# A two-layer hybrid decoder trunk: the mixer's side work in another order, and the first feed-forward's table work and transfers moved

## The chip, the cores and the metric

The kernel runs on one core of a Trainium2 chip. It is one launch. The metric is device microseconds (us) from start to end of it, and of several runs the median is taken.

## The reference

Everything is fp32: 256 positions, width 1024, two layers. What each layer computes:

```
x = x + 0.5 * swiglu(rms_norm(x, ffn1_norm), w_gate, w_up, w_down)      # D_FF = 2816
x = x + hybrid_mixer(rms_norm(x, mix_norm))
x = x + 0.5 * swiglu(rms_norm(x, ffn2_norm), w_gate2, w_up2, w_down2)

hybrid_mixer(h):
    proj = h @ w_in                 # splits: qkv, z, beta, a | s5_u | lru_x, lru_y | ret q, k, v, g | 4 gates of 1024
    A = gated delta rule (chunks of 64, a 64x64 triangular solve a head and chunk, a state of 64x64)
    B = s5_layer: complex diagonal scan over 16 groups of 64 states, gelu, then a GLU
    C = RG-LRU: a gated linear recurrence over 256 channels
    D = retention: rotary q and k, scores * decay mask, group norm, swish gate
    merged = sum_b sigmoid(gate_b) * (branch_b @ w_branch[b])
    return merged @ w_out
```

## The kernel before

The weights are what the time goes to. They arrive as some 400 pieces of 128x1024 (512 KB; some 448 KB) in HBM order of use. SyncE starts the transfer of piece i into one of three `raw` slots once VectorE has finished with piece i-3. ScalarE copies the piece, rounded to the matmul's format, into `whi` (L1026), VectorE writes the rest `raw - whi` into `wlo` (L1442; some late pieces go to GpSimd, L1357), and TensorE multiplies twice with `whi` and once with `wlo` (L487 to L489; the 16 units of gates L557 to L559, with 512 columns a matmul). So each piece takes about 2.7 us of TensorE, 1.0 of ScalarE and 1.2 of VectorE.

TensorE's order is written out by hand, and so are those of ScalarE and VectorE; the engines are in order, and each waits by semaphore counts. `split_to(i)` and `ahead(unit)` stand on ScalarE and VectorE for "bring the copies (or rests) up to piece i", so what is written between two of these delays the pieces behind it.

A layer has the stages FFN1 (22 units `gu1_0` to `gu1_21` of a gate and an up half, then `dn1`), the mixer (projections, gate units `g0` to `g15`, merges `mg0` to `mg7`, `wo`), and FFN2. FFN1 also carries work on the S5 parameters, which is small and dependent: four exponentials and an absolute value on ScalarE (L1139 to L1144, which need another activation table than silu does), a scan and two chains for an angle on VectorE, later the tables `tmpF`, `ret` of powers (`turn_tables`, L1583).

In the mixer the small matmuls of the four branches stand between gate units. Each writes one of four PSUM banks in the order of the table `SIDE`: a unit can only start when the unit four places earlier in the table was taken by the engine that the table names. The names used below: `eb`, `gb`, `bb` (decays and betas; L716, L734; taken as `dec` by VectorE L1800), `ktr`, `vtr` (transposed keys and values, L724, taken by VectorE L1778 to L1784), `kk`, `qk` (keys and queries against keys, L748, taken by VectorE L1816, L1819), `pq0` to `pq7` (input of S5's pairs of states, `s5_in`, taken by `s5_state` on VectorE, L1828 to L1837, then turned back on GpSimd, L1383 to L1387, and summed by `s5_out`), the units of the six levels of the triangular inverse (L815, L816 among them), `rotq`, `rotk`, `sc0` to `sc3`, `ro`, `rm`, `rv2` (rotation, scores, output, mean and variance of retention), `u`, `w`, `ws`, `su`, `oi`, `oa`, `gs` (delta rule; L893 is a product with new values, L1886 on VectorE makes these values).

Of the kernel before, what the change touches and what calls it, by code (L numbers as in the profile page):

```python
# [32 lines left out]
ALU = mybir.AluOpType  # L33
ACT = mybir.ActivationFunctionType
# [42 lines left out]
EARLY = CCOLS["bo"][0]  # L77

# [62 lines left out]
for _name, _n, _ in STREAM:  # L141
# [8 lines left out]
           if _n.startswith("mg") or _n in [f"g{_k}.1" for _k in range(11, 16)] + ["wo0.0", "wo1.0"]]  # L150
# [7 lines left out]
LEVEL_UNITS = ([[("x0_0", "act"), ("y0_0", "act"), ("x1_0", "act"), ("y1_0", "act"), ("t0_1", "act")]]  # L158
               + [[(f"{n}{hp}_{lv}", "act") for hp in range(2) for n in ("y", "xt")] for lv in range(1, LEVELS - 1)]
               + [[(f"yt0_{LEVELS - 1}", "act"), (f"y1_{LEVELS - 1}", "act")]])  # L160
SIDE = ([("lr", "act"), ("li", "act"), ("l2q", "act"), ("l2k", "act"), ("rowt", "act"), ("eb", "act"),
         ("ktr", "dve"), ("vtr", "dve")]
        + [("gb0", "dve"), ("bb0", "act"), ("gb1", "dve"), ("bb1", "act")]
        + [(n, "dve") for n in ("kk0", "kk1", "qk0", "qk1")]
        + [u for lv in range(LEVELS) for u in
           (LEVEL_UNITS[lv]
            + [(f"pq{s}", "dve") for s in ([2 * lv, 2 * lv + 1] if lv < 4 else [])]
            + ([("rotq", "dve"), ("rotk", "dve")] if lv == 4 else []))]
        + [("u", "act"), ("w0", "act"), ("w1", "act"),
           ("su0", "dve"), ("sc0", "dve"), ("sc1", "dve"),  # L170
           ("ws1", "dve"), ("oi1", "act"), ("su1", "dve"), ("sc2", "dve"), ("sc3", "dve"),
           ("ws2", "dve"), ("oi2", "act"), ("su2", "dve"), ("ro", "act"),
           ("ws3", "dve"), ("oi3", "act"), ("glu", "act"), ("rm", "dve"),
           ("oa0", "dve"), ("oa1", "dve"), ("gs", "act"), ("rv2", "act")])
# [43 lines left out]
def trunk(nc, weights, params, consts, positions, x_in, y_out):  # L218
    ctx = ExitStack()
    with ctx:  # L220
# [81 lines left out]
        scm = big[:, 16 * SEQ:16 * SEQ + 4 * 384].rearrange("p (h c) -> p h c", h=4)  # L302
# [158 lines left out]
        def sync_layer(sp):  # L461
            for i in range(max(Now.layer * NP, RAW_SLOTS), (Now.layer + 1) * NP):
                sp.wait_ge(*low_ready(i - RAW_SLOTS))
                sp.dma_start(landing(i), weight_piece(i)).then_inc(once[f"raw{i % RAW_SLOTS}"], 16)
                if i == 10:
                    sp.dma_start(par[:, NORMS:], layer_params(0)[:, NORMS:]).then_inc(S("par"), 16)
                if i == 16:
                    sp.dma_start(cst[:, EARLY:], consts[:, EARLY:]).then_inc(once["tables_load"], 16)
                if Now.layer + 1 < DEPTH and i == piece_at("dn2_0.0"):
                    sp.wait_ge(*since("hh", MF + MF // 2))  # L470
                    sp.wait_ge(*since("scaled", 2 * KD))
                    Now.layer += 1
                    sp.dma_start(par[:], layer_params(Now.layer)).then_inc(S("par"), 16)
                    Now.layer -= 1

        def tensor_layer(pe):
# [195 lines left out]
            pe.wait_ge(once["tables_load"], 16)  # L672
# [39 lines left out]
            ps = side_bank("eb")  # L712
            for t in range(2):
                for hp in range(2):
                    h = 2 * t + hp
                    last = mm(ps[64 * hp:64 * hp + 64, t * SEQ:(t + 1) * SEQ], ident[0:32, h:h + 1].to_broadcast([32, 64]), rows[0:32], start=True, stop=True)  # L716
            last.then_inc(S("side"), 1)
            gate(0)
            pe.wait_ge(S("k_normed"), 1)
            for unit, q0 in (("ktr", 2), ("vtr", 4)):  # L720
                ps = side_bank(unit)
                for j in range(2):
                    for t in range(2):
                        last = nc.tensor.transpose(ps[:, j * 256 + t * P:j * 256 + (t + 1) * P], qkv[:, q0 + t, j * P:(j + 1) * P], ident)  # L724
                last.then_inc(S("side"), 1)

            def decays_and_betas(hp):

                both = [(side_bank(f"gb{hp}"), 0), (side_bank(f"bb{hp}"), 32)]
                for t in range(2):  # L730
                    h = 2 * t + hp
                    for n, r in enumerate(chunks):
                        for ps, row in both:
                            last = mm(halves(ps[r, t * P:(t + 1) * P]), ident[row:row + 32, row + h:row + h + 1].to_broadcast([32, 64]),  # L734
                                      rows[row:row + 32].rearrange("p (j n c) -> p j n c", j=2, n=2)[:, :, n, :], start=True, stop=True)
                            if (t, n) == (1, 1):
                                last.then_inc(S("side"), 1)

# [12 lines left out]

            decays_and_betas(0)
            decays_and_betas(1)
            gate(1)
            against_k("kk", 2)
            against_k("qk", 0)
            gate(2)
            gate(3)
# [20 lines left out]

            pe.wait_ge(S("main_act"), main.taken("su"))  # L780
            def first_pair(hp):

                pe.wait_ge(S("y_first"), hp + 1)
                xs, ys = side_bank(f"x{hp}_0"), side_bank(f"y{hp}_0")
                for i in range(4):
                    t, j = i // 2, i % 2
                    for ps, swapped in ((xs, False), (ys, True)):
                        for r, out in zip(chunks, others):
                            if swapped:
                                last = mm(ps[out, i * 64:(i + 1) * 64], ident[r, r], mt[r, hp, t, j, :], start=True, stop=True)  # L790
                            else:
                                last = mm(ps[r, i * 64:(i + 1) * 64], mt[r, hp, t, j, :], ident[r, r], start=True, stop=True)
                        if i == 3:
                            last.then_inc(S("side"), 1)
# [33 lines left out]

            pe.wait_ge(once["masks"], 4)
            for hp in range(2):  # L830
                first_pair(hp)
                gate_part(4, hp)
            middle(side_bank("t0_1"), 0, 1, "x0_0")
            s5_in((0, 1))
            for lv in range(1, LEVELS - 1):
                gate_part(4 + lv, 0)
                ps = both_sides(0, lv, f"xt1_{lv - 1}" if lv > 1 else "t0_1")
                middle(ps, 1, lv, f"xt1_{lv - 1}" if lv > 1 else "x1_0")
                if lv >= 2:
                    s5_out(2 * lv - 4)  # L840
                    s5_out(2 * lv - 3)
# [3 lines left out]
                if lv < 4:  # L845
                    s5_in((2 * lv, 2 * lv + 1))
                if lv == 4:

                    pe.wait_ge(S("main_act"), main.taken("rv"))
                    for unit, src in (("rotq", rq), ("rotk", rk)):  # L850
                        ps = side_bank(unit)
                        for t in range(2):
                            last = mm(ps[:, t * SEQ:(t + 1) * SEQ], cst_("perm"), src[:, t, :], start=True, stop=True)
                        last.then_inc(S("side"), 1)
            lv = LEVELS - 1
            gate_part(4 + lv, 0)
            ps = side_bank(f"yt0_{lv}")
            inverse_rows(ps, 0, f"xt1_{lv - 1}")
            middle(ps, 1, lv, f"xt1_{lv - 1}")
            s5_out(2 * lv - 4)  # L860
            s5_out(2 * lv - 3)
            gate_part(4 + lv, 1)
            inverse_rows(side_bank(f"y1_{lv}"), 1, f"yt0_{lv}").then_inc(S("side"), 1)
            gate(10)

# [44 lines left out]
            def scores(h):  # L910
                t, r = h // 2, slice(64 * (h % 2), 64 * (h % 2) + 64)
                ps = side_bank(f"sc{h}")
                mm(ps[:, 0:SEQ], rk[r, t, 0:P], rq[r, t, :], start=True, stop=True)
                mm(ps[:, SEQ:384], rk[r, t, P:SEQ], rq[r, t, P:SEQ], start=True, stop=True).then_inc(S("side"), 1)

            def means(unit, src):

                ps = side_bank(unit)
                for t in range(2):
                    last = mm(ps[:, t * SEQ:(t + 1) * SEQ], bo, src[:, t, :], start=True, stop=True)  # L920
                last.then_inc(S("side"), 1)


            gate_part(11, 0)
            state_up(0)
            pe.wait_ge(S("rotated"), 2)
            scores(0)
            scores(1)
# [3 lines left out]
            scores(2)  # L932
            scores(3)
            gate_part(12, 0)
            from_state(2)
            state_up(2)

            pe.wait_ge(S("side_dve"), side.taken("sc3"))
            ps = side_bank("ro")
            for t in range(2):  # L940
                for j in range(2):
                    for hp, r in enumerate(chunks):
                        h = 2 * t + hp
                        v = slice(h * DH, (h + 1) * DH)
                        if j == 0:
                            mm(ps[r, t * SEQ:(t + 1) * SEQ], rv[:, 0, v], scm[:, h, 0:SEQ], start=True, stop=False)
                        else:
                            last = mm(ps[r, t * SEQ + P:(t + 1) * SEQ], rv[:, 1, v], scm[:, h, SEQ:384], start=False, stop=True)
            last.then_inc(S("side"), 1)
# [9 lines left out]
            pe.wait_ge(S("side_act"), side.taken("ro"))  # L959
            means("rm", tmpB)  # L960
# [13 lines left out]
            pe.wait_ge(S("ro_sq"), 1)  # L974
            means("rv2", tmpC)
# [33 lines left out]
        def scalar_layer(act):  # L1009
# [71 lines left out]
            def stack_masks():  # L1081

                act.wait_ge(once["tables_load"], 16)
# [52 lines left out]
            silus(1, range(0, 4))  # L1136
# [126 lines left out]
            ahead("g1")  # L1263
            for hp in range(2):
# [937 lines left out]
```

## Time and profile before

| what | value |
|---|---|
| time, median of 3 runs | 1316.59 us (1313.99 to 1317.89) |
| the profiled execution, its own time | 1312.74 us |
| its span | 1311.0 us |
| TensorE busy | 1281.6 us, 98% of the span |
| VectorE, ScalarE, GpSimd busy | 919.6, 673.2, 236.7 us |
| mean granted clock of TensorE | 0.994 of full speed |
| DMA | 220.14 MB, 168 GB/s on average |

The profile is of one execution, so its durations are compared with 1312.74 us, not with the median. Busy TensorE time counts matmuls that overlap, and includes stretches at half clock. The waits list says for which engine's instruction an idle engine waited.

### The profile page before, as it was taken

What the parts mean: (1) busy time and instruction counts of PE and PEld (TensorE: products, weight loads), DVE (VectorE), ACT (ScalarE), POOL (GpSimd) and SP (SyncE); (2) the same over time, 40 slices, a digit from 0 to 9 for tenths busy, and PEclk for the clock granted to TensorE, in tenths of its full rate; (3) what the DMA queues carried; (4) which work ended last, traced back from release to release, by engine and by line L of the source; (5) the groups of instructions that cost most, each with busy time, mean ns of one, the idle gap of its engine ahead of it and who ended that gap; (6) DMA issues with size and microseconds to landing.
All of it is one profiled execution on the core that took longest, in us unless ns stands there. A gap on an engine that the chain in (4) does not pass through costs nothing.

```text
span 1311.0 us, 25653 instructions
## 1 busy us (share of the span) xinstructions
PE 1281.6 (98%) x10848; PEld 1199.3 (91%) x10848; DVE 919.6 (70%) x1383; ACT 673.2 (51%) x991; POOL 236.7 (18%) x183
## 2 busy tenths in 40 slices
PE   9999999999999999999999999999999999999997
PEld 9999999987777899999999999999777778999997
DVE  5788675896967766666658885567879487566654
ACT  6544647654335465444554446477444445544542
POOL 1000011006834410000100000100366363000000
PEclk9999999999999999999999999999999999999999
DMA  6756564544242655566646556545423355555562
GB/s 204 245 186 194 183 200 145 166 149 141 86 139 99 178 175 194 187 211 209 193 147 200 175 187 206 170 154 169 159 85 113 97 161 186 166 189 185 173 218 91
DMA packets 92178, 220.14 MB, mean 168 GB/s; under 512 B 6944, under 2 KB 48160, under 8 KB 91680
## 3 DMA queue, kind: packets, MB, share of 16 engines
q1 hardware_dynamic: 92064, 218.50, 52.0%
q8 instruction: 86, 1.41, 0.4%
q14 instruction: 28, 0.23, 0.1%
HBM read 217.42 MB, written 1.05 MB: 167 GB/s over the span
## 4 chain that ended last, share of the span: by engine, by line
PE 79%; DVE 14%; ACT 3%; issue 2%; DMA 2%; POOL 0%; SPq 0%; DVEq 0%; ACTq 0%
PE bank L487 21%; PE bank L489 21%; PE bank L488 21%; DVE wlo L1442 4%; PE bank L557 3%; PE bank L558 3%; PE bank L559 3%; DMA raw<-weights 1%; DVE bank L1829 1%; DVE tmpA L1828 1%; PE bank L997 1%; PE bank L998 1%; PE bank L999 1%; ACT whi L1026 1%; DVE bank L1831 1%
## 5 line engine op out<-in xcount | busy, mean ns | idle before, releaser
L1442 DVE TENSOR_TENSOR wlo<-raw,whi 128x1024 fp32r<-128x1024 f32 (+1 forms) x384 | 475.1, 1260 | 237.4 <-ACT whi L1026 235.4
L1026 ACT ACTIVATE whi<-raw 128x1024 fp32r<-128x1024 f32 (+1 forms) x414 | 421.1, 1037 | 195.2 <-DMA raw<-weights 117.3
L487 PE MATMUL bank<-xh,whi 128*128 128x256 f32 x1744 | 489.2, 281 | 5.4 <-DVE wlo L1442 4.9
L488 PE MATMUL bank<-xl,whi 128*128 128x256 f32 x1744 | 486.8, 279 | 0.0
L489 PE MATMUL bank<-xh,wlo 128*128 128x256 f32 x1744 | 486.7, 279 | 0.0
L487 PEld LDWEIGHTS bank<-xh,whi 128*128 128x128 f32 x1744 | 327.8, 188 | 7.3 <-issue 6.7
L488 PEld LDWEIGHTS bank<-xl,whi 128*128 128x128 f32 x1744 | 327.8, 188 | 0.1
L489 PEld LDWEIGHTS bank<-xh,wlo 128*128 128x128 f32 x1744 | 327.8, 188 | 0.0
L487 PE MATMUL bank<-hh,whi 128*128 128x256 f32 x704 | 196.8, 280 | 0.0
L489 PE MATMUL bank<-hh,wlo 128*128 128x256 f32 x704 | 196.5, 279 | 0.0
L488 PE MATMUL bank<-hl,whi 128*128 128x256 f32 x704 | 196.5, 279 | 0.0
L1394 POOL TENSOR_TENSOR flat<-flat 128x256 f32<-128x256 f32 x36 | 35.6, 988 | 743.8 <-ACT flat L1052 742.9
L1110 ACT ACTIVATE tmpB<-tmpB 128x256 f32<-128x256 f32 x88 | 36.6, 417 | 219.3 <-DVE tmpB L1490 219.3
L487 PEld LDWEIGHTS bank<-hh,whi 128*128 128x128 f32 x704 | 132.3, 188 | 0.2 <-issue 0.2
L488 PEld LDWEIGHTS bank<-hl,whi 128*128 128x128 f32 x704 | 132.3, 188 | 0.0
L489 PEld LDWEIGHTS bank<-hh,wlo 128*128 128x128 f32 x704 | 132.3, 188 | 0.0
L557 PE MATMUL bank<-whi,xh 128*128 128x512 f32 x256 | 107.3, 419 | 2.1 <-DVE wlo L1442 2.1
L558 PE MATMUL bank<-wlo,xh 128*128 128x512 f32 x256 | 101.8, 398 | 0.0
L559 PE MATMUL bank<-whi,xl 128*128 128x512 f32 x256 | 101.6, 397 | 0.0
L1357 POOL TENSOR_TENSOR wlo<-raw,whi 128x1024 fp32r<-128x1024 f32 x30 | 73.7, 2469 | 73.6 <-ACT whi L1026 73.5
L1490 DVE TENSOR_TENSOR tmpB<-bank,invb 128x256 f32<-128x256 f32 x88 | 37.2, 423 | 58.1 <-PE bank L489 56.9
L557 PEld LDWEIGHTS bank<-whi,xh 128*128 128x128 f32 x256 | 48.6, 190 | 22.0 <-DVE wlo L1442 6.1
(408 smaller groups left out, 1558.1 us busy)
## 6 DMA issues: line engine op xcount, KB each, us to landing
raw<-weights SPq DMA_DIRECT2D x350, 512.0 KB, 3.8
raw<-weights SPq DMA_DIRECT2D x64, 448.0 KB, 4.0
cst<-consts SPq DMA_DIRECT2D x1, 1088.0 KB, 7.2
par<-params SPq DMA_DIRECT2D x1, 1072.5 KB, 7.2
par<-params SPq DMA_DIRECT2D x1, 1060.5 KB, 7.5
x<-x_in SPq DMA_DIRECT2D x2, 512.0 KB, 6.6
y_out<-ret SPq DMA_DIRECT2D x4, 256.0 KB, 2.1
ropec<-positions SPq DMA_DIRECT2D x1, 128.0 KB, 7.8
```

The source lines that it names most:

```text
L487: mm(out, w[0], a[0], start=start, stop=False)
L488: mm(out, w[0], a[1], start=False, stop=False)
L489: return mm(out, w[1], a[0], start=False, stop=stop)
L557: mm(in_four(ps), xh[:, k, t], wh[:, n, :], start=(k == 0), stop=False)
L558: mm(in_four(ps), xh[:, k, t], wl[:, n, :], start=False, stop=False)
L559: last = mm(in_four(ps), xl[:, k, t], wh[:, n, :], start=False, stop=(k == KD - 1))
L1026: A(slot(whi, i), slot(raw, i), ACT.Copy).then_inc(once["high"], 1)
L1110: A(tmpB[:, m % 2, :], tmpB[:, m % 2, :], ACT.Silu).then_inc(S(f"silu{f}"), 1)
L1357: tt(slot(wlo, i), slot(raw, i), r32(slot(whi, i)), ALU.subtract).then_inc(S("low_pool"), 1)
L1394: tt(squared[:, 0, :], squared[:, 0, :], squared[:, k, :], ALU.add).then_inc(S("sq_step" if k < KD - 2 else "sq_added"), 1)
L1442: V.tensor_tensor(slot(wlo, i), slot(raw, i), r32(slot(whi, i)), ALU.subtract).then_inc(S("low_dve"), 1)
L1490: V.tensor_tensor(tmpB[:, m % 2, :], main.bank(f"gu{f}_{m}")[:, 0:SEQ], invb, ALU.mult).then_inc(S("gated"), 1)
```

## The change

**Transfers.** In layer 0 the rest of the parameters (1060 KB in one transfer behind piece 10) and the tables (1088 KB in one transfer behind piece 16) are cut: the small parameters go behind piece 6, the rest in four parts behind pieces 12, 14, 16, 18, the tables in four parts behind 20, 22, 24, 26.

**FFN1.** ScalarE's exponentials stand one piece pair earlier, the last of them with the silu after it ahead of the pieces that it followed; the two angle chains on VectorE are interleaved; the powers (L1583) of part 1 are moved from before unit 13 into it, and later ones follow.

**Mixer.** The table `SIDE` and the written orders of TensorE, ScalarE and VectorE change together: decays before keys and values, S5's first pair ahead of gate unit 2, one state of S5 after each rest, retention's scores in level 5 and its output and norm right behind, the first and the last branch together.

The diff, cut to its core:

```diff
+LATE_PARAMS = _in_parts(12, 2, MATRICES, NPAR, 4)
+LATE_TABLES = _in_parts(20, 2, EARLY, NCST, 4)
...
-SIDE = ([("lr", "act"), ("li", "act"), ("l2q", "act"), ("l2k", "act"), ("rowt", "act"), ("eb", "act"),
-         ("ktr", "dve"), ("vtr", "dve")]
-        + [("gb0", "dve"), ("bb0", "act"), ("gb1", "dve"), ("bb1", "act")]
-        + [(n, "dve") for n in ("kk0", "kk1", "qk0", "qk1")]
...
+         ("gb0", "dve"), ("bb0", "act"), ("gb1", "dve"), ("bb1", "act"), ("ktr", "dve"), ("vtr", "dve")]
+        + [(n, "dve") for n in ("kk0", "kk1", "qk0", "qk1", "pq0", "pq1")]
...
@@ TensorE
-            decays_and_betas(0)
-            decays_and_betas(1)
             gate(1)
             against_k("kk", 2)
             against_k("qk", 0)
+            pe.wait_ge(S("main_act"), main.taken("su"))
+            s5_in((0, 1))
             gate(2)
             gate(3)
...
+            pe.wait_ge(S("rotated"), 2)
+            scores(0)
+            scores(1)
+            gate_part(9, 0)
...
+            scores(2)
+            scores(3)
+            gate_part(9, 1)
+            inverse_rows(side_bank("y1_5"), 1, "yt0_5").then_inc(S("side"), 1)
+            retained()
             gate(10)
+            pe.wait_ge(S("side_act"), side.taken("ro"))
+            means("rm", tmpB)
@@ ScalarE, FFN1
-            silus(1, range(0, 4))
+            silus(1, range(0, 3))
...
             A(ly_, lq, ACT.Exp, scale=-1.0).then_inc(S("pexp"), 1)
+            ahead("gu1_3")
             act.wait_ge(S("pmul"), 1)
             A(sm["mag"], sm["lrdt"], ACT.Exp).then_inc(S("pexp"), 1)
-            silus(1, range(4, 8))
+            silus(1, range(3, 8))
@@ VectorE, FFN1
             turn_tables(0)
-            turn_tables(1)
             for m in range(13, MF):
                 up(1, [m])
-                for part in {16: (5, 6), 17: (7,), 18: (8,), 19: (9, 10), 20: (11,), 21: ()}.get(m, (m - 11,)):
+                for part in {17: (5, 6), 18: (7,), 19: (8, 9), 20: (10, 11), 21: ()}.get(m, (m - 12,)):
                     turn_tables(part)
@@ VectorE, mixer
+            below(0)
+            below(1)
             dve.wait_ge(S("side"), side.ready("ktr"))
-            dve.wait_ge(S("side_act"), side.taken("rowt"))
...
             dve.wait_ge(S("tables"), 2)
+            s5_state(0)
             ahead("g3")
-            for lv in range(LEVELS):
-                for hp in range(2):
-                    split_to(last_piece(f"g{4 + lv}") + 2 + hp)
-                if lv < 4:
-                    s5_state(2 * lv)
-                    s5_state(2 * lv + 1)
...
+            s5_state(1)
+            for lv in range(LEVELS - 1):
+                split_to(last_piece(f"g{4 + lv}") + 2)
+                if lv < 3:
+                    s5_state(2 * lv + 2)
+                split_to(last_piece(f"g{4 + lv}") + 3)
+                if lv < 3:
+                    s5_state(2 * lv + 3)
+                if lv == 3:
+                    rotate()
...
             ahead("g11")
             state_up(0)
-            masked(0)
-            masked(1)
...
             values(1)
             state_up(1)
-            masked(2)
-            masked(3)
...
+            ahead("g14")
             link(V.tensor_tensor(go, go, tmpD, ALU.mult))
             link(V.scalar_tensor_tensor(go, go, gnh, zz, ALU.mult, ALU.mult))
             branch(0, go)
-            ahead("g14")
-
-            dve.wait_ge(S("side_act"), side.taken("rv2"))
-            link(V.reciprocal(tmpC, tmpC))
-            link(V.tensor_tensor(tmpB, tmpB, tmpC, ALU.mult))
```

How the rows of an engine stand, in the order in which it takes them (line numbers are those of each kernel; L1026 before is L1042 after, L1442 is L1464, L557 to L559 are L568 to L570). First ScalarE in FFN1 of layer 0, from the silu of unit 2 on. Before:

```order
L1110 ACTIVATE tmpB<-tmpB 128x256
L1104 ACTIVATE hh<-tmpC 128x256
L1026 ACTIVATE whi<-raw 128x1024 x2
L1110 ACTIVATE tmpB<-tmpB 128x256
L1104 ACTIVATE hh<-tmpC 128x256
L1139 ACT_TABLE_LOAD
...
L1142 ACTIVATE small<-small 128x2
L1144 ACTIVATE small<-small 128x8
L1026 ACTIVATE whi<-raw 128x1024 x2
L1110 ACT_TABLE_LOAD
```

And of the changed kernel, from the same silu:

```order
L1126 ACTIVATE tmpB<-tmpB 128x256
L1120 ACTIVATE hh<-tmpC 128x256
L1155 ACT_TABLE_LOAD
...
L1158 ACTIVATE small<-small 128x2
L1042 ACTIVATE whi<-raw 128x1024 x2
L1161 ACTIVATE small<-small 128x8
L1126 ACT_TABLE_LOAD
L1126 ACTIVATE tmpB<-tmpB 128x256
L1120 ACTIVATE hh<-tmpC 128x256
L1042 ACTIVATE whi<-raw 128x1024 x2
```

The first four exponentials and their table load moved from behind unit 3's silu to behind unit 2's, ahead of the copies of pieces 8 and 9; the last exponential, the load back and unit 3's silu now stand ahead of pieces 10 and 11.

Second TensorE in the mixer, from the small matmuls behind gate unit 0 to the start of gate unit 2. Before:

```order
L724 MATMUL bank<-cst,qkv 128x128 x8
L734 MATMUL bank<-rows,cst 64x128 x16
L557 MATMUL bank<-whi,xh 128x512
...
L559 MATMUL bank<-whi,xl 128x512
L748 MATMUL bank<-qkv 64x64 x32
L557 MATMUL bank<-whi,xh 128x512
```

And changed:

```order
L730 MATMUL bank<-rows,cst 64x128 x8
L749 MATMUL bank<-cst,qkv 128x128 x8
L568 MATMUL bank<-whi,xh 128x512
...
L570 MATMUL bank<-whi,xl 128x512
L761 MATMUL bank<-qkv 64x64 x32
L771 MATMUL bank<-su,par 128x256 x4
L568 MATMUL bank<-whi,xh 128x512
```

Half of the decay matmuls went ahead of gate unit 0, the other half ahead of the transposes, and the four matmuls of S5's first pair stand directly behind those of `kk` and `qk`.

Third VectorE in the mixer, from a rest of gate unit 1 on. Before (L1778 takes `ktr`, L1800 the decays, L1811 and L1812 mask them, L1816 and L1819 take `kk` and `qk`):

```order
L1442 TENSOR_TENSOR wlo<-raw,whi 128x1024
L1778 TENSOR_TENSOR qkvp<-bank,rowT 128x256
...
L1784 SCALAR_TENSOR_TENSOR qkvp<-bank,rowT 128x256 x2
L1442 TENSOR_TENSOR wlo<-raw,whi 128x1024
L1800 TENSOR_SCALAR big<-bank,rowT 128x64 x8
...
L1442 TENSOR_TENSOR wlo<-raw,whi 128x1024 x2
L1811 TENSOR_TENSOR big<-big,cst 128x256
...
L1816 SCALAR_TENSOR_TENSOR big<-bank,big 128x256 x2
L1819 TENSOR_TENSOR big<-bank,big 128x256 x2
L1442 TENSOR_TENSOR wlo<-raw,whi 128x1024 x6
```

And changed:

```order
L1464 TENSOR_TENSOR wlo<-raw,whi 128x1024
L1811 TENSOR_SCALAR big<-bank,rowT 128x64 x8
L1826 TENSOR_TENSOR qkvp<-bank,rowT 128x256
...
L1832 SCALAR_TENSOR_TENSOR qkvp<-bank,rowT 128x256 x2
L1464 TENSOR_TENSOR wlo<-raw,whi 128x1024
...
L1464 TENSOR_TENSOR wlo<-raw,whi 128x1024 x2
L1850 TENSOR_TENSOR big<-big,cst 128x256
...
L1855 SCALAR_TENSOR_TENSOR big<-bank,big 128x256 x2
L1858 TENSOR_TENSOR big<-bank,big 128x256 x2
L1464 TENSOR_TENSOR wlo<-raw,whi 128x1024 x2
L1867 TENSOR_TENSOR tmpA<-bank,wide 128x512
```

The eight instructions on decays moved from behind to ahead of those on `ktr` and `vtr`, and S5's first state stands after two rests where it stood after six.

## Rows read from the trace of the kernel before

**Rows 1.** The page: span, busy time of the engines, chain that ended last.
```profile
span 1311.0 us, 25653 instructions
...
PE 1281.6 (98%) x10848; PEld 1199.3 (91%) x10848; DVE 919.6 (70%) x1383; ACT 673.2 (51%) x991; POOL 236.7 (18%) x183
...
PE 79%; DVE 14%; ACT 3%; issue 2%; DMA 2%; POOL 0%; SPq 0%; DVEq 0%; ACTq 0%
```

**Rows 2.** Waits of TensorE: engine, line, waited for: total us, times, longest us.
```profile
PE bank L487 <- DVE wlo L1442: 4.9, 6, 1.8
PE bank L734 <- DVE qkvp L1784: 3.3, 2, 1.7
...
PE bank L893 <- DVE big L1886: 2.6, 2, 1.3
PE bank L557 <- DVE wlo L1442: 2.1, 3, 0.9
...
PE bank L815 <- DVE tmpC L1836: 0.4, 2, 0.2
```

**Rows 3.** TensorE in both FFN1: start, us, engine, line, op, tiles, count, [idle before, releaser].
```profile
42.48 0.35 PE L487 MATMUL bank<-xh,whi 128*128 128x256 f32 x1 [1.80 <-DVE wlo L1442]
...
93.66 0.35 PE L487 MATMUL bank<-xh,whi 128*128 128x256 f32 x1 [0.54 <-DVE wlo L1442]
...
686.01 0.36 PE L487 MATMUL bank<-xh,whi 128*128 128x256 f32 x1 [0.70 <-DVE wlo L1442]
...
738.07 0.36 PE L487 MATMUL bank<-xh,whi 128*128 128x256 f32 x1 [1.41 <-DVE wlo L1442]
```

**Rows 4.** Timeline of ScalarE at the parameter work of layer 0.
```profile
36.68 0.42 ACT L1110 ACTIVATE tmpB<-tmpB 128x256 f32<-128x256 f32 x1 [1.63 <-DVE tmpB L1490]
...
37.44 1.28 ACT L1139 ACT_TABLE_LOAD   x1
...
39.72 1.99 ACT L1026 ACTIVATE whi<-raw 128x1024 fp32r<-128x1024 f32 x2
```

**Rows 5.** Timeline of VectorE: parameter work (layer 0), turned tables (layer 1).
```profile
38.17 0.69 DVE L1558 TENSOR_TENSOR_SCAN tmpF<-cst 128x256 f32<-128x256 f32 x1 [0.87 <-DMA par<-params]
...
734.34 2.32 DVE L1583 TENSOR_SCALAR ret<-tmpF,small 128x256 f32<-128x256 f32 x8
```

**Rows 6.** Timeline of TensorE at the products of keys and queries, layer 0.
```profile
285.64 0.67 PE L734 MATMUL bank<-rows,cst 32*64 32x128 f32 x16 [1.65 <-DVE qkvp L1784]
...
292.04 1.16 PE L748 MATMUL bank<-qkv 64*64 64x64 f32 x64
```

**Rows 7.** Timeline of VectorE in the same stretch.
```profile
285.42 1.22 DVE L1442 TENSOR_TENSOR wlo<-raw,whi 128x1024 fp32r<-128x1024 f32 x1
...
290.01 2.35 DVE L1442 TENSOR_TENSOR wlo<-raw,whi 128x1024 fp32r<-128x1024 f32 x2
...
293.99 0.76 DVE L1816 SCALAR_TENSOR_TENSOR big<-bank,big 128x256 f32<-128x256 f32 x2
```

**Rows 8.** Timeline of VectorE: one level of the triangular inverse, beside GpSimd.
```profile
321.08 3.91 DVE L1442 TENSOR_TENSOR wlo<-raw,whi 128x1024 fp32r<-128x1024 f32 x2
```

**Rows 9.** Timeline of VectorE: delta-rule state and branch sums, layer 0.
```profile
385.72 2.30 DVE L1905 SCALAR_TENSOR_TENSOR tmpE<-tmpE,su 128x512 f32<-128x512 f32 x1
387.94 1.21 DVE L1442 TENSOR_TENSOR wlo<-raw,whi 128x1024 fp32r<-128x1024 f32 x1
...
411.31 3.42 DVE L1442 TENSOR_TENSOR wlo<-raw,whi 128x1024 fp32r<-128x1024 f32 x1
```

**Rows 10.** Windows of TensorE: us, busy (count), granted clock, DMA share, GB/s.
```profile
284.50:288.00 3.50, 2.35 (x24) 1.00 0.53 161
...
390.40:393.80 3.40, 3.40 (x19) 0.50 0.93 303
...
926.30:929.70 3.40, 1.74 (x29) 1.00 0.30 83
929.70:933.10 3.40, 3.40 (x22) 0.50 0.63 208
```

More of the change, by code:

```diff
@@ L737, in decays_and_betas @@
                                 last.then_inc(S("side"), 1)
+            ps = side_bank("eb")
+            for t in range(2):
+                for hp in range(2):
+                    h = 2 * t + hp
+                    last = mm(ps[64 * hp:64 * hp + 64, t * SEQ:(t + 1) * SEQ], ident[0:32, h:h + 1].to_broadcast([32, 64]), rows[0:32], start=True, stop=True)
+            last.then_inc(S("side"), 1)
+            decays_and_betas(0)
+            gate(0)
+            decays_and_betas(1)
+            pe.wait_ge(S("k_normed"), 1)
+            for unit, q0 in (("ktr", 2), ("vtr", 4)):
+                ps = side_bank(unit)
+                for j in range(2):
+                    for t in range(2):
+                        last = nc.tensor.transpose(ps[:, j * 256 + t * P:j * 256 + (t + 1) * P], qkv[:, q0 + t, j * P:(j + 1) * P], ident)
+                last.then_inc(S("side"), 1)
             def against_k(name, q0):
@@ L827, in inverse_rows, with rotated @@
                 return last
-            pe.wait_ge(once["masks"], 4)
[L830 to L834, printed above, removed]
+            def rotated():
+                pe.wait_ge(S("main_act"), main.taken("rv"))
+                for unit, src in (("rotq", rq), ("rotk", rk)):
+                    ps = side_bank(unit)
+                    for t in range(2):
+                        last = mm(ps[:, t * SEQ:(t + 1) * SEQ], cst_("perm"), src[:, t, :], start=True, stop=True)
+                    last.then_inc(S("side"), 1)
@@ new lines, in scores, with means @@
+            def scores(h):
+                t, r = h // 2, slice(64 * (h % 2), 64 * (h % 2) + 64)
+                ps = side_bank(f"sc{h}")
+                mm(ps[:, 0:SEQ], rk[r, t, 0:P], rq[r, t, :], start=True, stop=True)
+                mm(ps[:, SEQ:384], rk[r, t, P:SEQ], rq[r, t, P:SEQ], start=True, stop=True).then_inc(S("side"), 1)
+            def means(unit, src):
+                ps = side_bank(unit)
+                for t in range(2):
+                    last = mm(ps[:, t * SEQ:(t + 1) * SEQ], bo, src[:, t, :], start=True, stop=True)
+                last.then_inc(S("side"), 1)
@@ L931, in tensor_layer @@
             state_up(1)
-            scores(2)
-            scores(3)
             gate_part(12, 0)
             from_state(2)
+            pe.wait_ge(S("ro_sq"), 1)
+            means("rv2", tmpC)
             state_up(2)
[L938 to L949, printed above, removed]
             gate_part(12, 1)
@@ L1653, in vector_layer @@
             up(1, [11])
+            dve.wait_ge(once["tables_load"], TABLE_LOADS)
             cr, ci = halves(par_("scr"), 8), halves(par_("sci"), 8)
```

293 lines of the change are left out of this document (151 added, 142 removed).

## The prediction

> **What bounds the kernel now.** I read the page first [rows 1]: TensorE is busy 1281.6 of 1311.0 us, and four fifths of the chain that ended last are its matmuls. The change removes no matmul, so it can only move what TensorE waits for, and the half-clock stretches. Next the list of TensorE's waits [rows 2]: the reader is to see that no class is above 4.9 us, that the rests `wlo` from VectorE lead it, and that three classes lie where the change works: L734 behind the transposed values (3.3), L893 behind the delta rule's values (2.6), gates behind `wlo` (2.1). Then the timelines around each [rows 3 to 9], and the windows with the granted clock [rows 10]: behind some of these waits the clock stands at 0.50 for 3.4 us, and that is counted as busy. A dense stretch of 3.4 us at half clock does 1.7 us of work, so each costs up to 1.7 us, as much as the wait ahead of it.
>
> The sum is made against the profiled execution, 1312.74 us (span 1311.0 and 1.7 around it). It is 3.85 below the median 1316.59; I take the difference found in it off the median.
>
> **FFN1, ScalarE.** In layer 0 piece 10's rest holds TensorE up by 1.80 us until 42.48 [rows 3]. Its copy starts at 39.72, behind the table load of 1.28 at 37.44 and the five small functions, 2.28 in all [rows 4]. Afterwards load and four functions stand ahead of the copies of pieces 8 and 9. That shifts piece 8's rest to about 35.5, some 0.6 behind where TensorE wants it, a new wait. Then the last exponential needs the scan and a product on VectorE (scan 0.69, [rows 5]) behind gate and up of unit 3, so it comes at about 38.6; behind it now come the load back (1.28), the silu and its product (0.42 each, overlapping to 0.8 [rows 4]), and only then piece 10's copy, 40.7 to 41.6, and its rest until 42.9. So TensorE goes on at 43.03: 0.55 later than at present. In layer 1 the same order gives 687.05 for 686.01, +1.04.
>
> **FFN1, later.** In layer 1, eight L1583 take 2.32 us straight ahead of a rest for which TensorE waits 1.41 [rows 3, 5]. Four of the eight move behind it: half of 2.32 is 1.16; as a rest's start also frees the next transfer earlier, I take 1.2 to 1.57, -1.4. In layer 0 the wait of 0.54 at 93.66, goes, and with it 0.16 us of refilling (my value between nothing and the 0.35 that the first matmul takes [rows 3]): -0.70. FFN1 sum: 0.55 - 0.70 + 1.04 - 1.4 = **-0.5**. Interleaving the angle chains shortens VectorE's dependent work beside it, which TensorE doesn't wait for. The split transfers I cost at nothing: TensorE waits for no weight transfer there, and the tables' last part lands about 2 us before VectorE's first use. If that cover were gone, the price is up to a 1 MB transfer's worth of delay of that first use, some microseconds once; bounds 0 and +2.
>
> **Mixer, the decays.** Now VectorE takes `ktr` and `vtr`, and L734 waits 1.65 for it (1.66 in layer 1) until 285.64 [rows 2, 6]. With the decays split to both sides of gate unit 0, gate unit 1 can start at 285.4 instead of 286.2. But the eight decay instructions (some 1.6 us) now stand ahead of a rest that was done at 286.6 [rows 7] and will be at 288.4, when TensorE wants it at 288.3. So `kk` and `qk` end at 292.45 and not at 293.1.
>
> **Mixer, S5's first pair.** It needs the banks of `kk0` and `kk1`, four places earlier in the table. VectorE takes them in L1816, at 293.99 to 294.75 [rows 7], at the end of work without a gap: two rests until 292.3, four masks, then the pair. Nothing of that is moved away, and it starts 0.2 later. TensorE is there at 292.45 and the banks are free at 294.95, so it waits 2.6 us, where it now goes straight on with gate unit 2. Gate unit 2 starts at 296.2 for 293.1: +3.0, of which 1.06 are the four matmuls of the pair, moved from later. Net **+1.97** in layer 0. In layer 1 the present kernel has a half-clock window right behind the 1.66 wait (the one at 929.7 [rows 10]), which costs gate unit 1 some 1.1 and L734 0.46; the changed order breaks that wait up: net **+0.43**.
>
> **Mixer, the levels.** VectorE takes two rests in 3.91 us beside GpSimd's rotation back, against 1.21 for one alone [rows 8, 9]; L815 then waits 0.2 at a time, three times a layer [rows 2]. One state behind each rest spreads that; two waits of 0.3 remain by my replay. **-0.3** a layer (bounds -0.9 and +0.5). The Trainium skill, GPSIMD Engine Reference (the table of the engine's properties), says GpSimd's SBUF interfaces are shared with VectorE, with contention for instructions with two SBUF inputs. The trace agrees (`wlo` reads two: 3.91 against 2 x 1.21). By that rule respacing saves none of the stretching, only the queueing, and the sum would have 0 here in place of -0.3.
>
> **Mixer, state and retention.** At L893 TensorE waits 1.3 a layer for values that stand behind masks, L1905 (2.30, slowed) and a rest (1.21) [rows 2, 9]. The masks go to level 5 and L1905 behind the second values: -1.46 with the refill, +0.4 for small waits in the new order. Behind that wait comes a window at 0.50 (at 390.4 [rows 10]), and one alike in layer 1: -1.75 and -1.5. Sum **-2.8** and **-2.55**.
>
> **Mixer, the end.** A rest of 3.42 us beside GpSimd [rows 9] holds a gate up by 0.95 [rows 2]; a branch's six instructions ahead of it go behind the next one. **-1.1** a layer; my replay leaves it 0.5 us of margin.
>
> **Clock.** Does the new wait of 2.6 us bring a half-clock window of its own? For: windows with little work (1.74 of 3.40 busy, small matmuls) are followed by 0.50 [rows 10]. Against: 2.35 busy of 3.50 around the same kind of wait kept 1.00 [rows 10]; and the wait sits between dense gates. A window with 2.6 idle in it has less than either. It is not shown by any row, so from below 0, from above 1.7 a layer; between them I take 0.7, as one of two layers falls. The Trainium skill, TensorE: Matmul & The Clock Gate (Part 1, and its passage on oscillation), says that the throttled clock is the default, that activity releases it, and that waits between bursts bring it back. The trace agrees in kind (926.3, then 929.7 [rows 10]). By the rule alone both layers fall, which is the second rival below.
>
> Sum: FFN1 -0.5; layer 0: 1.97 - 0.3 - 2.8 - 1.1 = -2.2; layer 1: 0.43 - 0.3 - 2.55 - 1.1 = -3.5; clock +1.4 over both. **-4.8**, so 1316.6 - 4.8 = 1311.8.
>
> **Rivals.** (1) No new half-clock window: -6.2, 1310.4. For it speaks the 284.5 row; 0.22.
> (2) Both layers fall at full price (+3.4 for 1.4), and of what is removed about 1 us shows up again at the next unit, as TensorE is then nearer to VectorE's chain: -1.8, 1314.8, no change that can be told. The 926.3 row speaks for it; 0.20.
> (3) The banks are free in time, because VectorE's earlier work is drawn forward with the decays: the pair costs nothing, 2.6 less in each layer and no clock in question: about -10, 1306.5. Against it: VectorE's chain there has no gap [rows 7]; 0.08.
> (4) Slower. VectorE becomes the bound in the levels: L815 already waits 0.2 in those with two states [rows 2], so VectorE has nothing to spare there, and the new order puts rotation and scores into levels that were light. If every one of twelve levels takes x longer, the result is -4.8 + 12x; no gain from x = 0.4, slower by over 0.3% from x = 0.73. At x = 0.8 the time is 1316.6 + 4.8 = 1321.4. A rest slowed by 1.5 once per level [rows 8] would do it. Against: what waits there now is 0.2 a time, three times a layer, so x is so far 0.1 at most; 0.10.
> The forecast itself (one window falls) has 0.40.
>
> **Numbers.** 0.3% (3.95 us) is about what a measurement can tell: faster is below 1312.6. The forecast lies just below it, so 0.24 of its 0.40 go to faster, 0.16 to same. Rival 1 gives 0.18 to faster and 0.04 to same, rival 2 0.18 to same and 0.02 to slower, rival 3 0.08 to faster, rival 4 0.10 to slower. Faster 0.50, same 0.38, slower 0.12. The range leaves out half of rival 3 and most of rival 4, and takes in the bounds of transfers and levels: 1306.5 to 1318.5. The forecast's own is 1309.5 to 1314.
>
> **What would show it.** Right: S5's first pair (L771) waits about 2.6 us for L1855 in both layers; L893's successor, the product with new values, waits under 0.4; the gate at 414.8 has no wait; piece 10's copy in FFN1 comes behind the silu, and TensorE's wait there is some 0.6 plus 1.8; one window at 0.50 near the pair, none near the states. Wrong: no wait at L771; windows at 0.50 in the levels; L815-like rows that wait over 0.7 us in each level; a wait for the tables ahead of the scr products in FFN1.

## The result

The changed kernel takes 1318.56 us (median, 1312.8 to 1321.91, 18 runs) against 1314.89 of the kernel before (1310.6 to 1317.89, 18 runs): a ratio of 1.0025, 95% interval 1.0015 to 1.0035. It is 3.3 us slower, where 4.8 faster was forecast. The profiled execution took 1318.7, at its median; that of before (1312.74) had been 2.2 under its own.

The page of the changed kernel (span, busy time, chain that ended last), beside [rows 1]:

```profile
span 1316.6 us, 25674 instructions
...
PE 1278.7 (97%) x10848; PEld 1197.4 (91%) x10848; DVE 933.4 (71%) x1383; ACT 677.0 (51%) x995; POOL 236.0 (18%) x183
...
PE 78%; DVE 13%; ACT 4%; DMA 2%; issue 2%; POOL 0%; SPq 0%; DVEq 0%; ACTq 0%
```

TensorE is busy 2.9 us less and the span is 5.6 longer: the loss is idle time. VectorE is busy 13.8 us more with as many instructions. That is the clue: something made the same instructions longer. TensorE's waits, beside [rows 2] (who waited for what: total, times, longest):

```profile
PE bank L1013 <- DVE tmpA L2004: 7.3, 2, 3.7
PE bank L771 <- DVE big L1855: 5.0, 2, 2.5
PE bank L498 <- DVE wlo L1464: 4.7, 6, 1.5
...
PE bank L749 <- DVE big L1811: 1.4, 2, 0.9
PE bank L943 <- DVE big L1943: 1.3, 2, 0.7
...
PE bank L730 <- ACT egb L1279: 0.9, 1, 0.9
```

The waits at L734 and L815 are gone, though 1.4 comes back at the transposes (L749, behind the decays) and 0.9 once at L730, where L734 was; that of the values (L893 before, L943 now) fell from 2.6 to 1.3, S5's pair (L771) waits 2.5 a layer as worked out. But the first row is new and in no step of the prediction: 3.7 us a layer at a merge.

To see where time goes, the matmuls with weights are counted in both traces; their order is the same. Start of number k in us, before and changed, first layer:

```
   k   what                         before   changed  difference
   0   first                         10.64     10.17     -0.48
  75   early in FFN1                 20.69     20.71     +0.03
2160   gate unit 1                  286.24    285.30     -0.94
2184   gate unit 2                  293.13    296.46     +3.33
2190   six matmuls on               294.63    299.18     +4.55
2496   gate unit 15                 414.79    412.20     -2.59
2538   second half of merge 1       424.69    425.82     +1.13
2544   six matmuls on               426.09    428.55     +2.46
```

At gate unit 15 the changed kernel leads by 2.6 us, S5's wait and its half clock included (the 0.48 of the start is gone 75 matmuls on). Then it loses 5.05 within 48 matmuls, and the second layer repeats that (0.36 behind at the same gate, 5.40 forty-eight matmuls on, 5.59 at the end). The place, on VectorE:

```profile
408.75 1.22 DVE L1464 TENSOR_TENSOR wlo<-raw,whi 128x1024 fp32r<-128x1024 f32 x1
409.89 2.90 DVE L1988 TENSOR_TENSOR ly<-ly,tmpD 128x512 f32<-128x512 f32 x1
412.82 1.67 DVE L1989 SCALAR_TENSOR_TENSOR ly<-ly,small,zz 128x512 f32<-128x512 f32 x1
414.52 2.52 DVE L1835 CAST brh<-ly 128x512 fp32r<-128x512 f32 x1
417.07 2.79 DVE L1836 TENSOR_TENSOR brl<-ly,brh 128x512 fp32r<-128x512 f32 x1
419.78 2.63 DVE L1835 CAST brh<-tmpB 128x512 fp32r<-128x512 f32 x1
422.45 2.72 DVE L1836 TENSOR_TENSOR brl<-tmpB,brh 128x512 fp32r<-128x512 f32 x1
425.09 0.67 DVE L2004 SCALAR_TENSOR_TENSOR tmpA<-wide,bank 128x512 f32<-128x512 f32 x1
```

and on GpSimd in the same stretch (an `x2` or `x3` is a group):

```profile
409.58 2.65 POOL L1379 TENSOR_TENSOR wlo<-raw,whi 128x1024 fp32r<-128x1024 f32 x1 [7.20 <-ACT whi L1042]
412.19 1.74 POOL L1388 TENSOR_TENSOR brl<-tmpF,brh 128x512 fp32r<-128x512 f32 x1
413.90 5.42 POOL L1379 TENSOR_TENSOR wlo<-raw,whi 128x1024 fp32r<-128x1024 f32 x2
419.62 7.78 POOL L1379 TENSOR_TENSOR wlo<-raw,whi 128x1024 fp32r<-128x1024 f32 x3 [0.31 <-ACT whi L1042]
```

Read them in pairs: L1988 ends at 412.79, 0.56 behind the end of GpSimd's first (412.23); L1989 at 414.49, 0.56 behind 413.93; the last subtraction at 425.17, 0.55 behind the end of the second of GpSimd's three (424.62). One VectorE instruction goes through per GpSimd instruction. Before, four of the six began ahead of GpSimd's first and took their own time; the other branch's conversion met GpSimd and took 2.50 already then:

```profile
408.73 0.69 DVE L1936 TENSOR_TENSOR ly<-ly,tmpD 128x512 f32<-128x512 f32 x1
409.46 0.75 DVE L1937 SCALAR_TENSOR_TENSOR ly<-ly,small,zz 128x512 f32<-128x512 f32 x1
410.25 0.43 DVE L1787 CAST brh<-ly 128x512 fp32r<-128x512 f32 x1
410.70 0.69 DVE L1788 TENSOR_TENSOR brl<-ly,brh 128x512 fp32r<-128x512 f32 x1
...
411.06 2.59 POOL L1357 TENSOR_TENSOR wlo<-raw,whi 128x1024 fp32r<-128x1024 f32 x1 [8.93 <-ACT whi L1026]
```

That also accounts for VectorE's busy time: the six took 5.75 before and take 15.2 now, and the rest that took 3.42 takes 1.22, so 7.3 more a layer and 14.5 in both, against 13.8 for the whole kernel.

L2004 is what frees the first merge's bank. It stands behind both branches on VectorE, TensorE needs that bank (a ring of three) for the second half of merge 1 (`mg1`), and waits:

```profile
425.82 0.80 PE L1013 MATMUL bank<-whi,brh 128*128 128x512 f32 x1 [3.66 <-DVE tmpA L2004]
```

S5's pair, and windows of TensorE around it and around this wait (us, busy, granted clock, DMA):

```profile
295.08 1.45 PE L771 MATMUL bank<-su,par 32*128 32x256 f32 x8 [2.51 <-DVE big L1855]
...
294.60:298.00 3.40, 2.92 (x12) 0.67 0.44 146
298.00:301.40 3.40, 3.40 (x14) 0.83 0.76 232
...
422.40:425.80 3.40, 0.00 (x0) 0.95 0.51 159
425.80:429.20 3.40, 3.38 (x9) 0.55 0.62 189
```

Both waits are followed by a stretch at the lower level, in both layers. The 0.67 and 0.83 are one such stretch cut by the windows' edges: from 295.8 to 299.2 the granted clock is 0.50.

### The profile page after: what moved, and what is told of

It is laid out like the page before. It is cut to its first block, busy times and chain, and to the rows that moved or that the text cites. A ratio compares the mean times of both kernels' runs of the same rounds, so it can differ in the third digit from the quotient of the medians.

```text
span 1316.6 us, 25674 instructions
## 1 busy us (share of the span) xinstructions
PE 1278.7 (97%) x10848; PEld 1197.4 (91%) x10848; DVE 933.4 (71%) x1383; ACT 677.0 (51%) x995; POOL 236.0 (18%) x183
## 4 chain that ended last, share of the span: by engine, by line
PE 78%; DVE 13%; ACT 4%; DMA 2%; issue 2%; POOL 0%; SPq 0%; DVEq 0%; ACTq 0%
PE bank L498 20%; PE bank L500 20%; PE bank L499 20%; DVE wlo L1464 4%; PE bank L568 4%; PE bank L570 3%; PE bank L569 3%; DMA raw<-weights 1%; ACT whi L1042 1%; DVE qkv L1741 1%; DVE brh L1835 1%; PE bank L819 1%; PE bank L1013 1%; PE bank L771 1%; PE bank L1014 1%
## 5 line engine op out<-in xcount | busy, mean ns | idle before, releaser
L1464 DVE TENSOR_TENSOR wlo<-raw,whi 128x1024 fp32r<-128x1024 f32 (+1 forms) x384 | 471.1, 1249 | 233.5 <-ACT whi L1042 231.5
L1042 ACT ACTIVATE whi<-raw 128x1024 fp32r<-128x1024 f32 (+1 forms) x414 | 420.1, 1036 | 203.8 <-DMA raw<-weights 91.4
L568 PE MATMUL bank<-whi,xh 128*128 128x512 f32 x256 | 107.2, 419 | 1.0 <-DVE wlo L1464 0.9
L570 PE MATMUL bank<-whi,xl 128*128 128x512 f32 x256 | 102.2, 399 | 0.0
L568 PEld LDWEIGHTS bank<-whi,xh 128*128 128x128 f32 x256 | 48.9, 191 | 19.0 <-issue 4.9
```

Of the source, the lines that this page charges most:

```text
L568: mm(in_four(ps), xh[:, k, t], wh[:, n, :], start=(k == 0), stop=False)
L570: last = mm(in_four(ps), xl[:, k, t], wh[:, n, :], start=False, stop=(k == KD - 1))
L1042: A(slot(whi, i), slot(raw, i), ACT.Copy).then_inc(once["high"], 1)
L1464: V.tensor_tensor(slot(wlo, i), slot(raw, i), r32(slot(whi, i)), ALU.subtract).then_inc(S("low_dve"), 1)
```

## The experiments

The theory: VectorE's conversions, and its subtractions and products of two SBUF operands, wait for the GpSimd instruction in flight; the new order put six of them beside GpSimd's rests, so the first merge's bank comes free late. Rivals: order alone (too much work ahead of L2004), the FFN1 part, or S5's pair. Each ratio is to runs of the kernel before on the same chip.

**FFN1 part alone**: the kernel before with the diff's transfers and its FFN1 pieces on ScalarE and VectorE.

```diff
-                if i == 10:
+                if i in LATE_PARAMS:
...
-            silus(1, range(0, 4))
+            silus(1, range(0, 3))
```

> The kernel before with the change to FFN1 and the transfers alone, the mixer as it was. My sums: layer 0 -0.15, layer 1 -0.4 to -0.65, so about 0.5 to 0.8 us under before; TensorE's wait for the rest of piece 10 at 1.5 and a new one of 0.5 ahead of it, the wait at 93.7 gone. The rival, that the split transfers or the moved tables cost in layer 1 (the profile of the changed kernel has three waits of 0.3 to 0.9 early in the mixer of layer 1), expects +1 to +2 us and those waits again.

1313.45 us, 0.9990 (0.9976 to 1.0003) of before. The sum of -0.5 lies inside the interval (-3.2 to +0.4 us), +1 to +2 outside it. The early waits in layer 1's mixer are there too, but also in `before_halves` below, which has none of the change; they go with a weight transfer that took longer in those executions (ScalarE waited 3.31 and 2.79 for that piece, 1.95 in the kernel before, 3.34 in `transfers_alone` below). Why it took longer was not tried.

**Mixer part alone**: all other pieces of the diff, and none of these.

```diff
+            s5_in((0, 1))
             gate(2)
...
+            ahead("g14")
             link(V.tensor_tensor(go, go, tmpD, ALU.mult))
```

> The kernel before with the mixer's new order alone. If the loss is in the mixer's end and in S5's first pair, as the profile of the changed kernel says: a wait of 3.7 at the third merge and of 2.5 at S5's pair in each layer, each with a half-clock stretch behind it, and +3 to +5 us against before. If the FFN1 part makes the loss: no change to 2 us faster than before.

1318.89 us, 1.0031 (1.0017 to 1.0046): +4.1, with waits of 3.6 and 2.5 a layer at the two places. The loss is the mixer's.

**VectorE makes two more rests**, so GpSimd starts later.

```diff
-           if _n.startswith("mg") or _n in [f"g{_k}.1" for _k in range(11, 16)] + ["wo0.0", "wo1.0"]]
+           if _n.startswith("mg") or _n in [f"g{_k}.1" for _k in range(11, 14)] + ["wo0.0", "wo1.0"]]
```

> The changed kernel, but the rests of the pieces g14.1 and g15.1 are made by VectorE (2 x 1.2 us more a layer on it) and no longer by GpSimd, so that GpSimd stands still while VectorE works on the branches. My theory, that each of VectorE's conversions and subtractions waits there for the GpSimd instruction in flight: the six instructions that take 1.7 to 2.9 us go back to 0.4 to 0.8, the wait of 3.7 at the third merge is gone or below 1, and its half-clock stretch with it: 7 to 10 us faster than the changed kernel, about 4 to 7 faster than before. The rival, that the order of the work alone makes the third merge late (too much work on VectorE ahead of the first merged sum): the wait stays or grows by the 2.4 us more.

1307.83 us, 0.9954 (0.9938 to 0.9971): 6.0 under before, so 9.3 under the changed kernel by the two ratios. VectorE has 2.4 us a layer more to do, and the wait at the merge is gone. Four of the six are short again; the two that still meet GpSimd's rests of merges (411.22 to 413.69 and 414.81 to 417.28) are not:

```profile
411.35 2.89 DVE L1988 TENSOR_TENSOR ly<-ly,tmpD 128x512 f32<-128x512 f32 x1
414.27 0.75 DVE L1989 SCALAR_TENSOR_TENSOR ly<-ly,small,zz 128x512 f32<-128x512 f32 x1
415.06 2.51 DVE L1835 CAST brh<-ly 128x512 fp32r<-128x512 f32 x1
417.60 0.69 DVE L1836 TENSOR_TENSOR brl<-ly,brh 128x512 fp32r<-128x512 f32 x1
418.21 0.42 DVE L1835 CAST brh<-tmpB 128x512 fp32r<-128x512 f32 x1
418.66 0.69 DVE L1836 TENSOR_TENSOR brl<-tmpB,brh 128x512 fp32r<-128x512 f32 x1
```

The rival of too much work is refuted.

**S5's first pair behind gate unit 2**, its first state behind the rests that follow.

```diff
+            gate(2)
             pe.wait_ge(S("main_act"), main.taken("su"))
             s5_in((0, 1))
-            gate(2)
             gate(3)
...
-            s5_state(0)
             ahead("g3")
+            s5_state(0)
             s5_state(1)
```

> The changed kernel, with S5's first pair on TensorE behind gate unit 2 in place of ahead of it, and its first state on VectorE behind the rests of gate unit 3. The wait of 2.5 and the half-clock stretch behind it (1.6) should go in both layers: 6 to 8 us faster than the changed kernel. The rival, that TensorE then waits as long at the next unit, since VectorE's chain is late as a whole: under 2 us faster, and a new wait of 1 to 2.5 at gate unit 3 or in the first level.

1313.93 us, 0.9999 (0.9983 to 1.0014), so 3.4 under the changed kernel: between the two. The wait of 2.5 is gone, and part of it comes back in the first level, where the ring of banks wants the second state taken:

```profile
310.81 0.27 PE L800 MATMUL bank<-cst,big 64*64 64x64 f32 x2 [1.50 <-DVE tmpD L1875]
```

Behind this wait the granted clock stayed at 1.00 in layer 0 (310.8 to 317.6) and was 0.50 in layer 1 (954.2 to 957.6).

**GpSimd's rests in halves**: same elements, two instructions.

```diff
-                    tt(slot(wlo, i), slot(raw, i), r32(slot(whi, i)), ALU.subtract).then_inc(S("low_pool"), 1)
+                    n = slot(wlo, i).shape[-1] // 2
+                    tt(slot(wlo, i)[:, 0:n], slot(raw, i)[:, 0:n], r32(slot(whi, i)[:, 0:n]), ALU.subtract)
+                    tt(slot(wlo, i)[:, n:], slot(raw, i)[:, n:], r32(slot(whi, i)[:, n:]), ALU.subtract).then_inc(S("low_pool"), 1)
```

> The changed kernel, with each of GpSimd's rests made by two instructions of half the length. The same elements and bytes pass on GpSimd. My theory, that a conversion or subtraction of VectorE waits for the end of the one GpSimd instruction in flight: its time beside GpSimd falls from 2.5 to 2.9 to about 1.3 to 1.7 us, the six of them from about 15 to 9 us, and the wait of 3.7 at the third merge goes to nothing, -6 to -9 us against the changed kernel. The rival, that both engines share a port access by access: VectorE's instructions keep 2.5 to 2.9 us, the wait stays at 3.7 and the time within 1 us of the changed kernel.

1308.48 us, 0.9941 (0.9926 to 0.9956) of before, 11 under the changed kernel, more than the 6 to 9 expected. This tells the two forms of contention apart. VectorE in this kernel:

```profile
408.00 1.79 DVE L1990 TENSOR_TENSOR ly<-ly,tmpD 128x512 f32<-128x512 f32 x1
409.83 1.67 DVE L1991 SCALAR_TENSOR_TENSOR ly<-ly,small,zz 128x512 f32<-128x512 f32 x1
411.53 1.40 DVE L1837 CAST brh<-ly 128x512 fp32r<-128x512 f32 x1
412.97 1.67 DVE L1838 TENSOR_TENSOR brl<-ly,brh 128x512 fp32r<-128x512 f32 x1
```

and GpSimd:

```profile
407.73 1.51 POOL L1380 TENSOR_TENSOR wlo<-raw,whi 128x512 fp32r<-128x512 f32 x1 [6.10 <-ACT whi L1042]
409.21 1.73 POOL L1381 TENSOR_TENSOR wlo<-raw,whi 128x512 fp32r<-128x512 f32 x1
...
418.89 1.29 POOL L1380 TENSOR_TENSOR wlo<-raw,whi 128x512 fp32r<-128x512 f32 x1
```

The halves take 1.29 undisturbed and 1.5 to 1.75 beside VectorE, and TensorE now waits 0.6 twice for GpSimd's halves. Six instructions of VectorE take 9.7 us in place of 15.2, all of them done at 417.8 where it was 425.2, and the wait is gone.

**The first branch ahead of gate unit 15's rest again.**

```diff
-            ahead("g14")
             link(V.tensor_tensor(go, go, tmpD, ALU.mult))
             link(V.scalar_tensor_tensor(go, go, gnh, zz, ALU.mult, ALU.mult))
             branch(0, go)
+            ahead("g14")
             branch(3, tmpB)
```

> The changed kernel, with the first branch (product, norm, conversion, subtraction) ahead of gate unit 14's rest again, as before the change; GpSimd keeps its rests. Theory: of those four, two to three still meet GpSimd's instruction, which starts at 409.6, so the rest of g14.0 comes at 414 to 416 and is wanted at 412.2: the wait of 3.7 at the merge goes, one of 2 to 4 comes at gate unit 14; -1 to -5 us against the changed kernel. The rival, that the new place of the branch alone made the loss: no wait over 1 us at either place, -8 to -10 us.

(The rest that `ahead("g14")` brings is that of piece g15.0; the expectation calls it g14.0. Its "third merge" is the second half of merge 1.) 1324.21 us, 1.0057 (1.0040 to 1.0073): slower than the changed kernel, outside both expectations. Two instructions meet GpSimd, and the rest behind them too:

```profile
412.12 2.51 DVE L1835 CAST brh<-ly 128x512 fp32r<-128x512 f32 x1
414.66 1.63 DVE L1836 TENSOR_TENSOR brl<-ly,brh 128x512 fp32r<-128x512 f32 x1
416.22 3.36 DVE L1464 TENSOR_TENSOR wlo<-raw,whi 128x1024 fp32r<-128x1024 f32 x1
```

so gate unit 15 starts at 419.63 after a wait of 5.39. The mechanism was right and the size missed: I had not counted the slowed rest itself (2.1 us). So this part of the old order costs still more in the new surroundings. What differs from before is when GpSimd's rests fall: its first began 2.33 behind the branch's first product then (408.73 and 411.06), and 0.96 behind it here (410.61 and 411.57).

**Both cures together** (`own_rests` and `pair_later`).

> The changed kernel with VectorE making its own rests (as in own_rests) and S5's first pair behind gate unit 2 (as in pair_later). If the two are independent, the gains add: 1307.8 less 4 to 5, so 1303 to 1304.5, with the wait of 1.5 at the first level that pair_later showed. The rival, that VectorE becomes late at the end by the two rests more once TensorE is earlier: above 1306.

1304.99 us, 0.9913 (0.9897 to 0.9929): just above the expected 1303 to 1304.5. By the ratios 14.7 under the changed kernel, where 9.3 and 3.4 make 12.7: they add, within what the intervals can tell.

**S5's first state in VectorE's idle time**, as above but:

```diff
+            split_to(last_piece("g3") + 2)
             s5_state(0)
             ahead("g3")
             s5_state(1)
```

> As both, but S5's first state ahead of the rest of piece g4.1, where VectorE stands idle for 1.4 us in pair_later and which TensorE wants 3 us later. The wait of 1.5 at the first level should fall to about 0.5, and the half-clock stretch behind it (1.7) may go: 1300 to 1302. The rival, that any wait among those small matmuls brings the half clock: 1303, with a window at 0.50 there.

1303.12 us, 0.9899 (0.9882 to 0.9916). The wait at L800 is 0.7 once, in place of 1.5 twice; the time is 1 to 3 above what was expected. It is the rival's 1303, but without the rival's sign: the granted clock at these matmuls was 1.00, as it was in `both` behind its waits of 1.5. That this run is faster than `both` (0.9899 and 0.9913) is within the intervals.

**Halves in the kernel before**, with none of the change.

> The kernel before, with each of GpSimd's rests made by two instructions of half the length, and nothing of the change. If VectorE waits for GpSimd's instruction in flight there too, its rest of 3.42 at 411.3 falls to about 2 and the wait of 0.95 a layer goes: 1 to 3 us faster than before. Then the new order with the same cure (halves, 8.8 under before in its comparison) is worth 6 to 8 of it. The rival, that the shorter instructions alone are worth the 8.8: before_halves comes out 7 to 10 us faster as well.

1315.91 us, 0.9998 (0.9985 to 1.0011): no change, less than expected. The wait at gate unit 15 goes, but the merge waits 0.7 twice in its place, and matmuls wait 0.7 twice for GpSimd's halves (L1359):

```profile
PE bank L487 <- DVE wlo L1444: 5.0, 6, 2.1
PE bank L734 <- DVE qkvp L1786: 3.3, 2, 1.7
...
PE bank L997 <- DVE tmpA L1962: 1.5, 2, 0.7
PE bank L487 <- POOL wlo L1359: 1.3, 2, 0.7
```

So the halves are worth nothing without the new order, and with it 11 us: they undo a loss that the new order made. The new order with this cure gains about 8 us (0.9941).

**Halves and S5's state in the idle time**: the changed kernel with the edits of `halves` and `pair_mid_own`, without VectorE's two further rests.

> The changed kernel with S5's first pair behind gate unit 2 and its first state ahead of the rest of g4.1 (as in pair_mid_own), and GpSimd's rests in halves in place of VectorE making two of them. Both cures of the late branches gave the same time to 1 us (1307.8 and 1308.5, in two comparisons), so 1302.5 to 1305. A rival: GpSimd's halves are slower together (1.5 and 1.7 beside VectorE) and hold up the merges once TensorE is earlier (waits of 0.6 for GpSimd's rests): 1305 to 1307.

1300.94 us, 0.9889 (0.9870 to 0.9908): the best of all, 15 us under before, and under the 1302.5 to 1305 expected, which is not explained; the rival's waits of 0.6 for GpSimd's rests are there (1.3 in all), its time is not. Its list of waits has no L771, L800, L943 or L1013:

```profile
PE bank L498 <- DVE wlo L1466: 4.0, 5, 1.5
PE bank L498 <- DVE mgl L2016: 2.8, 2, 1.4
PE bank L518 <- DMA cst<-consts: 2.8, 1, 2.8
PE bank L568 <- DVE wlo L1466: 2.0, 6, 0.5
```

**Split transfers alone.** The parameters and tables in parts, no computing instruction moved.

> The kernel before with the split transfers alone, every instruction of the four computing engines where it was. The prediction costed them at nothing: within 1 us of before, the same waits. A rival: the parts are in the way of weight transfers, or free them, by more than 1 us, with another set of waits for rests in FFN1 of layer 0.

1314.95 us, 0.9995 (0.9981 to 1.0009): nothing that can be told.

## Why the prediction was wrong

- **The step that failed** is "Mixer, the end": "-1.1 a layer; my replay leaves it 0.5 us of margin". The -1.1 came: gate unit 15 starts at 412.20 without a wait. But the replay took the branch's instructions at the durations they had ahead of GpSimd's work (0.43 to 0.75), in a place where GpSimd works. They took 1.7 to 2.9, 15.2 us for the six, and cost 3.66 of waiting, the refill, and 1.3 of half clock: 5.05 a layer, 10.1 in all. With that, -4.8 becomes +5.3, against 5.6 between the two profiled spans. The runs show it twice over: taking GpSimd out of the way gives back 9.3, GpSimd's shorter instructions 11.
- **Luck in the sum.** The other terms came out near the forecast -4.8 (5.6 less 10.1 is -4.5) only by cancelling. The clock cost 1.8 more than I had, and the waits of 0.65 and 0.88 early in layer 1's mixer were in no term. Against that, from the seventh matmul of gate unit 2 to gate unit 15 the two layers gained 7.1 and 7.0, where my terms (the pair's 1.06 back, levels, states, end) make 5.3 and 5.0. Which of levels, states and retention gave the rest was not tried.
- I had the mechanism in hand and priced it only in the levels. The Trainium skill, GPSIMD Engine Reference (table of the engine's properties), names VectorE's two-port modes beside instructions with two SBUF inputs. The trace agrees: the conversion reads one SBUF operand and takes 2.52 beside GpSimd for 0.43 alone. What counts is where each such instruction lands against GpSimd's, not how many there are.
- **Rival 4** had the right sign and engine, and the wrong place: no level waits 0.7. VectorE became the bound behind gate unit 15.
- **S5's first pair**: right. 2.51 waited for 2.6, and gate unit 2 at 296.46 for 296.2, behind L1855 in both layers.
- **Clock**: mis-sized. I took one layer of two to fall; both did, at about 1.6 us each (gate unit 2's first six matmuls already lose 1.2), so +3.2 for +1.4. The second rival's bound was nearer, and so was the Trainium skill, TensorE: Matmul & The Clock Gate (Part 1): waits between bursts bring the lower level back. The traces agree nearly always: five profiled executions have this wait of 2.5 in both layers, and half clock follows nine of the ten (the exception is layer 0 of `halves`, at 1.00).
- **State and retention**: right in kind. The wait fell from 1.3 to 0.64, where I had named under 0.4 as the sign, and no half-clock window lies behind it. The 1.75 and 1.5 for half clock were read from one execution, and the first is not sure: in layer 0, behind the same wait of 1.3, the clock was 0.50 in the kernel before and `ffn_alone` and 1.00 in `before_halves` and `transfers_alone`; in layer 1 it was 0.50 in all four.
- **FFN1**: right within what can be told. Piece 10's wait is 1.54 behind a new one of 0.52 (0.6 forecast), the one at 93.7 is gone. **Transfers**: right, nothing.
- The chances: 0.12 for slower by over 0.3%; the measured 0.25% lies within "same" (0.38), but its interval leaves out 1, and 1318.56 is just outside the range. The base was 1316.6 by three runs; by 18 it is 1314.89. Rival 3's sum was wrong: -4.8, less 2.6 twice, less the clock's 1.4 is -11.4, not -10; nothing else rests on it.

## What to carry to other kernels

When an instruction is moved, take its duration from rows beside the same neighbours on other engines, not from where it stood. Where VectorE's busy time grows with the same count of instructions, look for one engine's instructions ending just behind another's; shorter instructions on the slower engine then helped here as much as moving its work away (0.9941 and 0.9954, intervals overlapping). A half-clock stretch read from one execution is not a fixed price: look at several. And a change that looks spent may hide a gain: here some 10 us of loss at one merge covered 8 of gain.

## What the runs showed of the hardware

- Beside a GpSimd subtraction of 128x1024 (2.40 us undisturbed, 2.5 to 2.85 beside VectorE), VectorE's products, subtractions and conversions of SBUF operands that began within it ended behind its end: those of 128x512 by 0.55 for products and subtractions (0.69 to 0.75 alone, 1.6 to 2.9 here) and by 0.28 for conversions (0.43 alone, 2.5 to 2.6 here), a rest of 128x1024 by 1.08 (1.22 alone, 3.4 here). Each of these is the instruction's time alone less 0.14 to 0.2.
- Not slowed: L2009, a sum with one PSUM operand, took 0.69 at 431.04, within GpSimd's instruction of 429.99 to 432.39; a reciprocal of one SBUF operand took 3.34 at 414.66 in the kernel before, with GpSimd at work, and 3.35 at 405.34 without.
- With GpSimd's instructions halved, VectorE's fell to 1.4 to 1.8: they wait for the instruction in flight, and GpSimd's wait too (1.29 undisturbed, 1.47 behind a conversion, 1.73 to 1.75 behind a subtraction or product). That the two take turns is how I read it; a port was not measured.
- A wait of 5.39 us of TensorE, with dense gates on both sides, was followed by matmuls of 0.63 for 0.40 at a granted clock of 0.50; in the window behind the one of 3.66 the granted clock was 0.55. Behind shorter waits it differed between executions and layers: 2.51 nine times of ten, 1.3 in layer 0 twice of four.
